# A hybrid decoder block on one core: another order in the opening, in the softmax mixer and ahead of the summed products, and other pages for the mixers' first parts

## What is computed

```
h = layer_norm(x)
proj = h @ w_in          # q, f, i, gate of mixer A; q, k, v, f of mixer B; gate_a, gate_b
y_a = hgrn2_branch(...)  # 4 heads of 128, gated linear recurrence
y_b = fox_branch(...)    # 8 heads of 64, causal softmax attention with a decay bias
merged = sigmoid(gate_a) * (y_a @ w_a) + sigmoid(gate_b) * (y_b @ w_b)
h = layer_norm(alpha * h + merged @ w_o)
ff = square(relu(h @ w_ff1)) @ w_ff2
ple = sigmoid(h @ w_pg) * (p @ w_p)
out = layer_norm(alpha * h + ff + ple)
```

## Time and profile before

| what | us |
|---|---|
| median of 3 runs (lowest, highest) | 1726.96 (1726.82, 1730.2) |
| the profiled execution | 1726.71 |
| its span in the profile | 1724.2 |
| PE, DVE, ACT, POOL busy | 1633.9, 1072.9, 700.6, 663.2 |
| mean granted clock of TensorE | 0.991 of full |

### The profile page before, as it was taken

How to read it: one execution, slowest core, us unless ns; L and a number is a source line. 1 busy time by engine, 2 the same in 40 slices (tenths; PEclk the granted TensorE clock), 3 DMA queues, 4 the chain that set the end, 5 groups by cost and what they waited for, 6 DMA issues and landing times.

```text
span 1724.2 us, 21211 instructions
## 1 busy us (share of the span) xinstructions
PE 1633.9 (95%) x8016; PEld 1357.2 (79%) x8016; DVE 1072.9 (62%) x1641; ACT 700.6 (41%) x1070; POOL 663.2 (38%) x470
## 2 busy tenths in 40 slices
PE   4999999999989899999999979999999999999997
PEld 3888887877767778878878768788888888888886
DVE  7547987534555540006615568988666579966977
ACT  2144453235777760012032453354544553343332
POOL 3132122321324233333444268676556513323334
PEclk9999999999999999999999989999999999999998
DMA  8111000111010211111134443455344398868672
GB/s 273 72 50 37 25 25 25 37 38 37 9 42 25 62 50 49 49 49 49 49 122 125 144 135 125 166 201 187 135 155 168 134 312 265 266 195 243 207 220 98
DMA packets 207924, 200.77 MB, mean 116 GB/s; under 512 B 8520, under 2 KB 178760, under 8 KB 205776
## 3 DMA queue, kind: packets, MB, share of 16 engines
q1 hardware_dynamic: 204656, 188.35, 35.0%
q10 hardware_dynamic: 3168, 11.08, 1.7%
HBM read 153.23 MB, written 46.17 MB: 116 GB/s over the span
## 4 chain that ended last, share of the span: by engine, by line
PE 78%; DVE 8%; ACT 5%; issue 5%; DMA 2%; SPq 1%; POOL 1%; DVEq 0%; ACTq 0%; POOLq 0%
PE dense L831 9%; PE dense L833 9%; PE dense L835 9%; PE dense L1111 3%; PE dense L1112 3%; PE dense L1113 3%; PE dense L1191 3%; PE dense L1192 3%; PE dense L1193 3%; PE mixA L941 3%; ACT parts L1431 2%; PE mixA L1111 2%; PE mixA L1112 2%; PE mixA L1113 2%; PE mixB L1111 2%
## 5 line engine op out<-in xcount | busy, mean ns | idle before, releaser
L831 PE MATMUL dense<-parts 128*128 128x512 f32 x880 | 301.5, 412 | 13.0 <-ACT page L1303 4.2
L833 PE MATMUL dense<-parts 128*128 128x512 f32 x880 | 285.1, 394 | 0.0
L835 PE MATMUL dense<-parts 128*128 128x512 f32 x880 | 283.9, 392 | 0.0
L740 POOL CAST parts<-page 128x1024 fp32r<-128x1024 f32 x55 | 60.3, 1096 | 441.3 <-PE dense L835 335.8
L743 POOL TENSOR_TENSOR parts<-page,parts 128x512 fp32r<-128x512 f32 x134 | 190.5, 1442 | 48.0 <-ACT parts L1495 43.6
L835 PEld LDWEIGHTS dense<-parts 128*128 128x128 f32 x880 | 166.2, 189 | 37.0
L833 PEld LDWEIGHTS dense<-parts 128*128 128x128 f32 x880 | 166.0, 189 | 35.3
L831 PEld LDWEIGHTS dense<-parts 128*128 128x128 f32 x880 | 155.0, 191 | 40.7 <-issue 14.3
L805 POOL TENSOR_TENSOR parts<-page,parts 128x512 fp32r<-128x512 f32 x52 | 88.8, 1729 | 207.4 <-ACT parts L1606 207.4
L780 POOL TENSOR_TENSOR page<-page 128x512 f32<-128x512 f32 x80 | 122.7, 1534 | 64.2 <-PE dense L1113 26.4
L788 POOL TENSOR_TENSOR parts<-page,parts 128x512 fp32r<-128x512 f32 x80 | 112.9, 1414 | 57.7 <-ACT parts L1542 52.5
(11 more groups left out here) (242 smaller groups left out, 3742.0 us busy)
## 6 DMA issues: line engine op xcount, KB each, us to landing
page<-in_w_ff SPq DMA_DIRECT2D x104, 512.0 KB, 5.8
page<-act_scratch SPq DMA_DIRECT2D x56, 512.0 KB, 5.6
page<-in_w_in SPq DMA_DIRECT2D x90, 256.0 KB, 3.3
act_scratch<-page SPq DMA_DIRECT2D x16, 1024.0 KB, 4.0
act_scratch<-page SPq DMA_DIRECT2D x16, 768.0 KB, 7.0
page<-in_w_o SPq DMA_DIRECT2D x32, 256.0 KB, 3.2
h_scratch<-page ACTq DMA_DIRECT2D x8, 512.0 KB, 2.7
page<-c_scratch SPq DMA_DIRECT2D x8, 512.0 KB, 5.0
```

Of the source, the lines that this page charges most:

```text
L831: mm(o, whi, x_, start=first, stop=False)
L833: mm(o, whi, x_, start=False, stop=False)
L835: ins = mm(o, wlo, x_, start=False, stop=last)
```

## The change

1. *Opening.* DVE makes all four low parts of the first weight pages. Its order is: statistics and norm of tile 0, low parts of weights 0 and 1, low part of tile 0, low parts of weights 2 and 3, statistics and norm of tile 1; then for each t: statistics of t+1, low part of t, norm of t+1. ACT copies the high part of tile 0 between weights 1 and 2. PE turns tile t+1 inside value job t (behind k = 5 of the first, k = 3 of the others).
2. *Softmax mixer.* DVE does the maximum ahead of the low part, ACT the scaling ahead of the copy.
3. *Pages.* The parts of y_a and y_b go to lists of pages; the first two of y_a to pages 50 to 53, which held scores' operands, and their copies don't wait for the last gate.
4. *Last merged tile.* Low part of tile 6 ahead of B7; tile 7 is multiplied, added, copied and split by halves. The second half of the output jobs waits for the right half.
5. *Sums.* POOL's and ACT's work for tiles 6 and 7 is interleaved with weight sums of pair 0; DVE's t1, t2 and t4 of tile 7 read PSUM and don't wait for ACT's raw copy, which now waits for them; early_low(3, 1) moves behind token_sums(6).

```diff
-PG_YAH, PG_YAL, PG_YBH, PG_YBL = 11, 15, 19, 23
+PG_YAH, PG_YAL, PG_YBH, PG_YBL = (50, 51, 13, 14), (52, 53, 17, 18), (19, 20, 21, 22), (23, 24, 25, 26)
+T_HI = [(6, 0), (6, 1), (7, 0), (7, 1), (6, 2), (6, 3), (7, 2), (7, 3)]
...
         def _(pool):
-            for j in (2, 3):
-                pool.wait_ge(w0_hi, j + 1)
-                nc.gpsimd.tensor_tensor(R(WLO + j), F(PG_W0 + j), R(WHI + j).bitcast(F32),
-                                        ALU.subtract).then_inc(w0_split, 1)
...
-            for q in range(NPAIRS):
+            weight_sum(0, 5)
+            weight_sum(0, 6)
+            token_sum(6)
+            sum_low(0, 5)
+            token_low(6, 0)
+            token_low(6, 1)
+            weight_sum(0, 3)
+            sum_low(0, 6)
+            token_low(6, 2)
+            weight_sum(0, 7)
+            sum_low(0, 3)
+            token_low(6, 3)
+            sum_low(0, 7)
+            for q in range(1, NPAIRS):
...
@@ tensor
+                    if between and between[0] == k:
+                        between[1](t + 1)
...
+            turn_tokens(0)
+            for t in range(TT):
+                pe.wait_ge(h_split, t + 1)
+                value_job("vhg", t, (3 if t else 5, turn_tokens))
...
+                    if h and m == 0:
+                        pe.wait_ge(m_split, KD + 1)
...
@@ scalar
                 nc.scalar.copy(R(WHI + j), F(PG_W0 + j)).then_inc(w0_hi, 1)
-            for t in range(TT + 1):
+                if j == 1:
+                    tokens_high(0)
+            rstd_estimate(1)
+            for t in range(1, TT + 1):
                 if t + 1 < TT:
                     rstd_estimate(t + 1)
                 if t < TT:
+                    tokens_high(t)
...
+                if 1 <= G < 65:
+                    g = G - 1
+                    x_ = F(PG_XP + g % 2, 0, (g % 8 + 1) * P)
+                    act.wait_ge(rinv_ready, g + 1)
+                    A(x_, x_, ACT.Identity, scale=rinv[:, g % 2, :]).then_inc(p_scaled, 1)
                 if 2 <= G < 66:
                     g = G - 2
                     act.wait_ge(p_turned, g + 1)
...
-            done(act, "gx", 15)
             for k in range(4):
-                nc.scalar.copy(R(PG_YAH + k), F(PG_YA + k)).then_inc(y_hi, 1)
+                if k == 2:
+                    done(act, "gx", 15)
+                nc.scalar.copy(R(PG_YAH[k]), F(PG_YA + k)).then_inc(y_hi, 1)
...
+                if t == TT - 1:
+                    act.wait_ge(t_sum, 11)
                 nc.scalar.copy(x_raw[:, :, cols], mixed).then_inc(h1_raw, 1)
...
+            last_high(6, 0)
+            last_high(6, 1)
+            weight_high(0, 5)
+            last_high(7, 0)
+            last_high(7, 1)
             h1_high(7)
...
+            weight_high(0, 6)
+            for t, n in T_HI[4:]:
+                last_high(t, n)
+            weight_high(0, 3)
             weight_high(0, 7)
...
@@ vector
+            for t in range(1, TT):
                 if t + 1 < TT:
+                    tokens_stats(t + 1)
+                tokens_low(t)
+                if t + 1 < TT:
+                    tokens_norm(t + 1)
...
                     V.reciprocal(rinv[:, g % 2, :], psm[:, g % 4, :]).then_inc(rinv_ready, 1)
-                if 2 <= G < 66:
-                    g = G - 2
...
-                    V.tensor_tensor(pt_part(g, True), mixB[:, 0:L].rearrange("q (j n) -> q j n", n=P),
-                                    pt_part(g, False).bitcast(F32), ALU.subtract).then_inc(pt_split, 1)
                 if G < 64:
                     hh, L = G // 8, (G % 8 + 1) * P
                     dve.wait_ge(qk_done, G + 1)
...
                     V.tensor_scalar(nmx[:, G % 2, :], mx[:, G % 2, :], -1.0, None, ALU.mult).then_inc(nmx_ready, 1)
+                if 2 <= G < 66:
+                    g = G - 2
...
+                if m == KD - 1:
+                    merged_low(m - 1, whole, m)
+                done(dve, "B", m)
...
+                    for hf, cols in enumerate(halved):
+                        ins = V.tensor_tensor(t2[:, cols], out_of("B", m)[:, cols], F(PG_GB[m])[:, cols], ALU.mult)
...
+                        V.tensor_tensor(t1[:, cols], t1[:, cols], t2[:, cols], ALU.add).then_inc(m_sum, 1)
+                    for hf, cols in enumerate(halved):
+                        merged_low(m, cols, KD + hf)
...
-                dve.wait_ge(h1_raw, t + 1)
+                if t < TT - 1:
+                    dve.wait_ge(h1_raw, t + 1)
+                else:
+                    dve.wait_ge(h1_raw, 4)
+                    dve.wait_ge(h1_turned, t + 1)
...
-                    elif t == 7:
-                        early_low(3, 1)
                     token_sums(t - 1)
...
                 elif t == 7:
+                    early_low(3, 1)
                     early_low(3, 2)
```

More of the change, by code:

```diff
@@ L746, in _, with token_sum @@
             PT = nc.gpsimd.tensor_tensor
-            for t in range(4, TT - 1):
+            def token_sum(t):
                 tt = slice((t - 4) * P, (t - 3) * P)
@@ L873, in _, with value_job @@
             h_lo_p = [R(XLO + k) for k in range(KD)]
-            def value_job(name, t):
+            def value_job(name, t, between=None):
                 j = JOB[name, t]
@@ L1048, in _ @@
                 for name, hi, lo, first in (("A", PG_YAH, PG_YAL, 0), ("B", PG_YBH, PG_YBL, 4)):
-                    for _ in feature_job((name, m), first * P, P, [R(hi + k) for k in range(4)],
-                                         [R(lo + k) for k in range(4)],
+                    for _ in feature_job((name, m), first * P, P, [R(k) for k in hi], [R(k) for k in lo],
                                          (y_split, lambda k: first + k + 1) if m == 0 else None):
@@ L1258, in _ @@
                 if t < TT:
[L1259 to L1264 removed]
+                    tokens_high(t)
+                store_values(PG_VHG, "vhg", t - 1, 0)
             def neg_exp(page, sem_, *name):
@@ L1457, in _ @@
             for k in range(4):
-                nc.scalar.copy(R(PG_YBH + k), F(PG_YB[k])).then_inc(y_hi, 1)
-            for m in range(KD):
+                nc.scalar.copy(R(PG_YBH[k]), F(PG_YB[k])).then_inc(y_hi, 1)
+            for m in range(KD - 1):
                 act.wait_ge(m_sum, m + 1)
                 nc.scalar.copy(R(PG_GA[m]), F(PG_M1 + 2 * (m % 2))).then_inc(y_hi, 1)
+            for hf in range(2):
+                act.wait_ge(m_sum, KD + hf)
+                nc.scalar.copy(R(PG_GA[KD - 1], hf * HALF, HALF),
+                               F(PG_M1 + 2 * ((KD - 1) % 2), hf * HALF, HALF)).then_inc(y_hi, 1)
             nc.scalar.preload_act_table_set("natural_log_exp_and_others")
@@ L1960, in _, with merged_low @@
             dve.wait_ge(gx_exp, 16)
[L1961 to L1968 removed]
+            def merged_low(i, cols, n):
+                dve.wait_ge(y_hi, 8 + n)
+                V.tensor_tensor(R(PG_GB[i])[:, cols], F(PG_M1 + 2 * (i % 2))[:, cols], R(PG_GA[i])[:, cols].bitcast(F32),
+                                ALU.subtract).then_inc(m_split, 1)
+            whole, halved = slice(0, 1024), (slice(0, HALF), slice(HALF, 1024))
+            for m in range(KD):
+                t1, t2 = F(PG_M1 + 2 * (m % 2)), F(PG_M2 + 2 * (m % 2))
+                if m >= 2:
+                    dve.wait_ge(m_split, m - 1)
+                done(dve, "A", m)
+                V.tensor_tensor(t1, out_of("A", m)[:, :], F(PG_GA[m]), ALU.mult).then_inc(a_used, 1)
+                if m == KD - 1:
+                    merged_low(m - 1, whole, m)
+                done(dve, "B", m)
+                if m < KD - 1:
                     V.tensor_tensor(t2, out_of("B", m)[:, :], F(PG_GB[m]), ALU.mult).then_inc(b_used, 1)
```

148 lines of the change are left out of this document (73 added, 75 removed).

## The result

The changed kernel takes **1736.0 us** (median of 5 runs, 1734.1 to 1739.3) where the kernel before takes 1729.8 beside it (1726.8 to 1730.8). The ratio is 1.0042, with a 95% interval of 1.0026 to 1.0058: slower by more than the 0.2% that counts as a difference here. The forecast was 1727.5 and no difference. The time itself lies in the range given (1716 to 1737).

A forecast was written before the change was run, and what follows sets the result against it. TensorE, busy in 95% of the span, was taken as the bound, with time to come only from its waits and half clock. Terms +3.6 +11.5 -3.0 -3.5 -7.8 = +0.8 on the profiled 1726.7 gave 1727.5 us, range 1716 to 1737.

The forecast's parts named there:

- Opening: First token tiles: earlier first value job, but a slower loop per tile; net loss +3.6 us, bounds -1 and +5.
- closed loop of 7.3 us a tile: First token stage: statistics, estimate, copy, low part and norm set 7.3 us per tile, where turns show 6.34.
- Rival C: First token stage: ACT's estimate doesn't hold the copy, opening worth -0.7, total 1723.2 us; chance 0.12.
- Softmax mixer: Eight heads: loop of scores, maximum, low part, weighing and turn takes 30.8 us against 29.2; +11.5, bounds +4 to +15.
- discount from near 13 to 11.5: Softmax mixer: near 13 us for eight heads cut to 11.5, as TensorE itself sets some steps of small tiles.
- term 2: Softmax mixer's two new orders: +11.5 us, said to be unable to come out under its loop; bounds +4 to +15.
- Rival B: Softmax mixer: the exponential's chain set the head, so -13.6 in place of +11.5, total 1702.4 us; chance 0.08.
- Other pages: First mixer projection: 2.5 us wait and 1.5 half clock go, less 1.0 for late parts; -3.0, bounds -1 to -4.
- Halves: Last merged tile, first output job: 1.8 us wait and 1.3 of half clock go; -3.5, bounds -2 to -3.8.
- Weight sums: Summed products: 8.0 us wait for POOL and its half clock go, two waits of 1 to 2 return; -7.8.
- Rival D: Summed products: POOL gates the first two weight pairs, weight sums give 5, total 1730.3 us; chance 0.15.
- rival A: Softmax mixer also loses its clock, 1.5 us a fall: 1733.5 with one in half the heads, 1739.5 in all; chance 0.15.

## Why the prediction was wrong

The mechanisms were right in the main, the sum was not. That 1736.0 still lies in the range is owed to the range's width of 21 us. Term by term, forecast against the table of borders:

- **Opening, +3.6 forecast, +2.95 measured.** The closed loop of 7.3 us a tile is there (7.30), and the estimate is its link (moving it gives 3.5). One item of its count is off: 2.44 less 1.1 plus 0.21 is 1.55, not 1.45. The first value matmul came at 21.86 (forecast 22.2), but this was luck: the forecast counted from a turn that is over at 17.4, and the turn was over at 14.0, with the copy held by the second weight page instead. Rival C is out.
- **Softmax mixer, +11.5 forecast, +15.7 measured: this is the step that failed.** The loop is the right one, as four experiments show: the cost comes and goes with the two orders, it comes with DVE's and not with ACT's, and it turns into a gain when TensorE issues the scores first. Two sizes were off. The loop was reckoned at 30.8 us a head and measured 31.1; it left out that the low part waits for ACT's copy in some steps, 6.1 us of all, which would cover the difference (not tried by itself). The statement that whatever ACT does is beside the loop was wrong to that extent. And the discount from near 13 to 11.5, because "some steps of small tiles are set by TensorE itself either way", has no row behind it: all seven distances from the first turn of one head to that of the next grew, by 1.4 to 2.1 us, 1.9 on average. Eight heads at 1.9 are 15.2, the rest is at the ends. The growth is not even within a head: of the eight distances from one step's last scores matmul to the next one's, the first two became 0.85 and 0.42 us shorter (on average of the heads two to seven), the third hardly changed (+0.1), and the five others grew by 0.3 to 1.0. So steps that don't lose do exist. But a step that something else than the loop sets can only be longer than the loop's length, never shorter, so such steps are no reason to go under the loop's 30.8 for the head. The forecast said itself that term 2 "cannot come out under the loop", and then went under it. Rival B (faster) is out.
- **Other pages, -3.0 forecast, -2.6 measured alone.** The two new waits are there, 0.55 and 0.68. The 1.5 us for the half clock should not have been added to the wait: in the kernel before it lay over two such waits, and without it they stand there by themselves, as the run with the weight sums alone shows. By the same run the 1.0 us taken off for late third and fourth pages was no loss of the change either, since 0.51 and 0.58 stand there without it. Two errors of 1.5 and 1.0 nearly cancelled, which is luck. The term is then 2.5 us of wait and little else.
- **Halves, -3.5 forecast.** With the pages the two gave 5.6 in the changed kernel, so about 3.0 fall to the halves. They were not run alone. The forecast of no wait in the output job was wrong by 0.43.
- **Weight sums, -7.8 forecast, -6.2 measured (-6.0 alone).** The 8.0 us wait went as forecast, and so did the two waits that come back (1.52 and 1.37, "1 to 2" forecast). But the fifth summed product, where the forecast made its sum, came 6.8 us earlier and not 7.8; the other 0.5 goes up between it and the 21st, where no term looked. For the 1.0 us POOL's prices are to blame. In the changed kernel its operations here take 1.26 to 1.29 us when no DVE operation with two inputs from SBUF is under way at their start, 1.73 to 1.75 when one is, and 1.53 to 1.56 when that one ends soon after:

```profile
1041.03 1.73 POOL L783 TENSOR_TENSOR page<-page 128x512 f32<-128x512 f32 x1
1042.72 1.26 POOL L791 TENSOR_TENSOR parts<-page,parts 128x512 fp32r<-128x512 f32 x1
```

  Thirteen of them lie between 1031.3 and 1051.3, 1.54 on average. I had taken 1.5 for the early and 1.35 for the late ones, and named twelve operations; at these prices twelve end by 1034.2, and the 1035.5 needs the thirteen of the trace. One DVE operation beside costs POOL 0.47 us, not the half of 0.6 that I read out of the row of four. That row hid it: one by one its four operations take 1.30, 1.75, 1.71 and 1.71, the first with no such DVE operation under way. The rule of the Trainium skill (SBUF — State Buffer, "Who interferes with whom") would have made this term -6.3, and the runs gave -6.2 and -6.0: here the page was nearer than my reading of the row. At the fifth product itself, for which both sums were made, the 6.8 lies between the two. Single rows fit such an exclusion: DVE's low part from 1039.84 on took 1.78 us and not 0.68, and POOL's operation begun beside it at 1041.03 ends 1.14 us behind it, about the 1.26 that it takes alone. Rival D named the direction.
- **The sum.** +0.8 forecast, +8.6 at the end of the summed products: 4.2 from the softmax mixer, 1.6 from the weight sums, 0.9 from the pages and halves, 1.45 between the first job and the first scores and 0.3 later, which no term had, less 0.65 from the opening. Between the medians the difference is 6.2, since the profiled execution of the kernel before is a quick one of its kind (1726.7 against a median of 1728.6 to 1729.8 in every later set).

The chances leaned the same way as the sum: "slower" had 0.31, and most of that through rival A and the spread of term 2. A bound of +15 for term 2 with +11.5 taken was the choice to question. The loop itself said near 13, and nothing measured stood behind the discount. It is 1.5 of the 4.2 us that term 2 missed by; without it the forecast would have been 1729.0, still no difference.

## What to carry to other kernels

When two engines hand results to each other in a fixed order, write down the closed loop through both queues. An operation moved ahead on one engine helps only if the engine that feeds it and the one that waits behind it issue their parts in the matching order; here the same two orders cost 16 us with the scores issued last, and left the mixer 5.7 us shorter than before with the scores issued first. And a loop's length times its number of turns is the forecast: don't discount it for steps that seem to be free unless a row shows them so. When a row merges several operations, look at them one by one before you take their mean as a price.

## What the runs showed of the hardware

- **The half clock of TensorE is no fixed cost of a wait.** Behind the same wait of 2.49 us ahead of the first projection the granted clock was 0.50 in two profiles (the kernel before; the two softmax orders alone) and 1.00 in a third (the weight sums alone), with the same code there. The 320 us from the job behind the token stage to the first scores, which no edit here touches, took 319.4 to 322.7 us in fourteen profiles. All of those over 321 have either a stretch at 0.50 that begins between 364.7 and 368.9, or one near 291 to 300 that is twice as long as in the others. The one from 365 on stands in seven of the ten profiles with the new opening and in none of the four with the old; what decides it was not tried and stays open. The Trainium skill (TensorE: Matmul & The Clock Gate, Part 1) says of the rise at a kernel's start that its place varies from run to run of the same kernel. These profiles, one each of fourteen kernels, show the like in the middle of a stretch of unchanged code.
- **The clock decides the opening as well.** The first value job starts at 21.86 in the changed kernel and at 21.56 with the softmax orders put back, but the third turn comes at 35.58 and 34.06. The granted clock rises to 1.00 at 27.0 in the one and at 24.4 in the other, and TensorE's matmuls of the first job shorten from 0.63 to 0.40 us there; what that gives is kept through the stage (81.18 against 79.67).
- **DVE and POOL hold each other up in both directions.** DVE's low parts of a token tile, with two inputs from SBUF, took 1.12 to 1.78 us beside POOL in the changed kernel, and 1.77 for the one that was moved to DVE. One of that size took 0.68 with POOL idle (at 1012.13 in the kernel before), and those with one input in PSUM took 0.68 to 0.69 beside POOL.
